# Low parts of the queries formed from the SBUF copy, and one weight split moved a step later, in a one-core decoder step

## What is computed

```python
def nsa_query_side(x, g_pre, w_in):
    u = rms_norm(x, g_pre) @ w_in
    q = u[..., :Q_WIDTH].reshape(b, t, KV_HEADS, GROUP, HEAD_DIM)
    z = u[..., Q_WIDTH:Q_WIDTH * (1 + N_BRANCH)].reshape(b, t, N_BRANCH, N_HEADS, HEAD_DIM)
    gate = jax.nn.sigmoid(u[..., Q_WIDTH * (1 + N_BRANCH):]) ...
    return q, z, gate

# per branch: compressed, selected, window
o = softmax(q k * scale + bias, masked) v          # and y = sum(gate * o * silu(z)) @ w_out
```

## Time and profile before

| | |
|---|---|
| median of three runs | 906.84 us (906.04 to 906.98) |
| span of the profiled execution, first to last instruction | 902.7 us |
| TensorE busy | 870.8 us (96%) |
| VectorE busy | 555.0 us (61%) |
| ScalarE busy | 453.1 us (50%) |
| GpSimd busy | 301.5 us (33%) |
| mean granted TensorE clock | 0.996 |

### The profile page before, as it was taken

One profiled execution on the slowest core, in us unless ns is written; L12 is line 12 of the kernel. 1 busy time (PEld: TensorE's weight loads), 2 busy tenths in 40 slices (PEclk: granted clock), 3 DMA queues, 4 the chain that ended last, 5 costly groups with the idle time before them and its releaser, 6 DMA issues.

```text
span 902.7 us, 16743 instructions
## 1 busy us (share of the span) xinstructions
PE 870.8 (96%) x6226; PEld 754.9 (84%) x6226; DVE 555.0 (61%) x1206; ACT 453.1 (50%) x919; POOL 301.5 (33%) x311
## 2 busy tenths in 40 slices
PE   5999999999999999999999999999999999899996
PEld 4999999946888787779989898989899998786664
DVE  6479999998966772223245555556464645635564
ACT  6567777535544542224446565555564545523231
POOL 2398988797220000003023232323323232500000
PEclk9999999999999999999999999999999999999999
DMA  9365333137178292337323222222322002923521
GB/s 257 97 184 152 102 102 85 40 96 230 42 258 333 107 299 53 105 56 208 95 44 74 48 71 49 70 63 58 69 65 54 25 1 48 276 90 99 184 84 36
DMA packets 158165, 99.52 MB, mean 110 GB/s; under 512 B 97202, under 2 KB 147026, under 8 KB 158005
## 3 DMA queue, kind: packets, MB, share of 16 engines
q1 hardware_dynamic: 143278, 79.30, 32.9%
q0 software_dynamic: 4896, 10.32, 3.2%
q10 hardware_dynamic: 9911, 8.84, 2.9%
HBM read 89.58 MB, written 18.85 MB: 120 GB/s over the span
## 4 chain that ended last, share of the span: by engine, by line
PE 87%; DVE 4%; ACT 4%; issue 3%; ACTq 1%; POOL 1%; DVEq 0%; POOLq 0%
PE psum L2264 8%; PE psum L2265 7%; PE psum L2266 7%; PE psum L1925 6%; PE psum L1927 6%; PE psum L1926 6%; PE psum L2359 6%; PE psum L2117 5%; PE psum L2116 5%; PE psum L2003 5%; PE psum L2118 5%; PE psum L2310 4%; PE psum L2327 3%; PE psum L1906 2%; PE psum L2292 2%
## 5 line engine op out<-in xcount | busy, mean ns | idle before, releaser
L810 ACT ACTIVATE arena<-psum 128x256 f32<-128x256 f32 (+9 forms) x230 | 90.3, 430 | 178.3 <-PE psum L2266 66.2
L2264 PE MATMUL psum<-u_hi,tile_hi 128*128 128x288 f32 x464 | 143.3, 309 | 4.6 <-ACT arena L810 2.2
L789 POOL TENSOR_SCALAR arena<-arena,kept 128x512 f32<-128x512 f32 (+3 forms) x128 | 83.5, 670 | 176.8 <-DVE kept L1762 176.8
L2265 PE MATMUL psum<-u_lo,tile_hi 128*128 128x288 f32 x464 | 137.4, 296 | 0.0
L2266 PE MATMUL psum<-u_hi,tile_lo 128*128 128x288 f32 x464 | 136.4, 294 | 0.0
L1434 DVE SCALAR_TENSOR_TENSOR psum<-arena,psum 128x512 f32<-128x512 f32 x168 | 127.0, 756 | 6.0
L1925 PE MATMUL psum<-h_hi,tile_hi 128*128 128x288 f32 x352 | 104.3, 296 | 0.0
L1926 PE MATMUL psum<-h_lo,tile_hi 128*128 128x288 f32 x352 | 103.8, 295 | 0.0
L1927 PE MATMUL psum<-h_hi,tile_lo 128*128 128x288 f32 x352 | 103.8, 295 | 0.0
L2264 PEld LDWEIGHTS psum<-u_hi,tile_hi 128*128 128x128 f32 x464 | 87.3, 188 | 10.4 <-ACT arena L810 4.1
L1256 ACT ACTIVATE arena<-arena,kept 128x512 f32<-128x512 f32 (+3 forms) x128 | 70.5, 552 | 45.0 <-DVE kept L1728 44.2
(11 more groups left out here) (318 smaller groups left out, 1902.8 us busy)
## 6 DMA issues: line engine op xcount, KB each, us to landing
tile_whole<-in_b_w_in SPq DMA_DIRECT2D x64, 256.0 KB
tile_whole<-in_a_w_in SPq DMA_DIRECT2D x24, 512.0 KB
arena<-in_cmp_w SPq DMA_DIRECT2D x4, 2048.0 KB, 10.3
kvw_whole<-in_w_kv SPq DMA_DIRECT2D x6, 1024.0 KB, 14.2
bias_copies<-bias_line POOLq DMA_DIRECT2D x4, 1280.0 KB, 23.6
arena<-in_x_prompt SPq DMA_DIRECT2D x8, 512.0 KB, 6.4
kvw_whole<-in_a_w_out SPq DMA_DIRECT2D x4, 1024.0 KB, 11.3
arena<-bias_copies SPq DMA_DIRECT2D x16, 256.0 KB, 4.0
```

Of the source, the lines that this page charges most:

```text
L789: pool.tensor_scalar(L, L, rden[:, stat(n) + k:stat(n) + k + 1], gR[:, i, h:h + 1], ALU.mult, ALU.mult).then_inc(S["pn_ready"], 1)
L810: return nc.scalar.activation(out, in_, ACT.Copy, scale=scale)
L2264: pe.matmul(pb(7, HT), w_hi, u_hi[:, k, here], start=(k == 0), stop=False)
L2265: pe.matmul(pb(7, HT), w_hi, u_lo[:, k, here], start=False, stop=False)
```

## The change

Four edits:

- `q_full` moves to another place in SBUF and is 576 columns wide instead of 512, so that it also holds the sampled queries. ScalarE's copy of the second half is 288 columns wide (it was 224). Before it writes, ScalarE also waits until VectorE has finished with the queries of the group before.
- VectorE forms `q_lo` as `q_full - q_hi`, both in SBUF, with a tensor_tensor; it was a scalar_tensor_tensor on bank 7 and `q_hi`. The sampled queries too come from `q_full`.
- `bank_read`: after a half of the queries bank 7 counts as read when ScalarE has written `q_hi`; it counted as read when VectorE had written `q_lo`, and after the second half also the sampled queries.
- The loop that starts `split_lo`: nothing at position 0; at position 1 the split that stood at the end of position 0. The other splits stay.

```diff
-        q_full = at(R_H + 2560, SEQ)
+        q_full = at(R_H + 2432, NT)
...
-            return ("qk_lo", q_low(n, hf)) if kind == "q" else ("zb_ready", 3 * n + (3 if hf else 1))
+            return ("qk_hi", 6 + 2 * (n - 1) + hf + 1) if kind == "q" else ("zb_ready", 3 * n + (3 if hf else 1))
...
                     act.wait_ge(S["s_done"], UPM * (n - 1) + 1)
-                    copy(q_full[:, here], pb(7, here.stop - here.start), QSCALE)
+                    act.wait_ge(S["qk_lo"], q_low(n, 0) - 1)
+                    copy(q_full[:, hf * HT:hf * HT + HT], pb(7, HT), QSCALE)
                     copy(q_hi[:, n % 2, here], pb(7, here.stop - here.start), QSCALE).then_inc(S["qk_hi"], 1)
...
-                q_rest(q_lo[:, m % 2, here], pb(7, here.stop - here.start), q_hi[:, m % 2, here])
+                V.tensor_tensor(out=q_lo[:, m % 2, here], in0=q_full[:, here], in1=q_hi[:, m % 2, here],
+                                op=ALU.subtract).then_inc(S["qk_lo"], 1)
                 if hf:
-                    q_samples(m, pb(7, HT)[:, SEQ - HT:HT], QSCALE)
+                    q_samples(m, q_full[:, SEQ:NT], 1.0)
...
-                for i in tiles_over(n - 1):
+                for i in tiles_over(n - 2) if n % 5 == 1 else tiles_over(n - 1) if n % 5 else ():
                     if i + HRING < N_TILES:
                         split_lo(i + HRING + 1)
```

## The result

The changed kernel takes 920.53 us (median of 5 runs, 920.37 to 923.95) against 906.08 us for the kernel before, in runs on the same chip (5 runs, 903.77 to 906.98). The ratio is 1.0169 (1.015 to 1.0187): slower by 1.7%, clear of its interval, and 1 us beyond the upper end of the predicted range. The profiled spans differ by 15.9 us, where the sum had 9.2. A run's time lies 1.8 us above its span (920.37 against 918.6), not 4.1 us as taken ahead of the prediction; by that, as an estimate, the profiled execution of the kernel before took 904.5 us, 2.3 us under the median of 906.84. The forecast adds to that median and doesn't depend on it.

What follows compares the result with a forecast made beforehand. TensorE, busy 870.8 of 902.7 us, was taken as the bound. Six groups at +1.8 - 0.18 us less 0.5 for group 0 gave +9.2, span 911.9, plus 4.1 to the median: 916.0 us, range 909.5 to 919.5.

Steps and rivals of the forecast that it cites:

- the sum: Whole kernel: +9.7 us for groups 1 to 6 and -0.5 us for group 0, together +9.2 us on the span.
- The bank stops being a limit: Positions 2 and 3, first tile parts: bank 7 clears earlier, saving 0.30 and 0.18 us in each of seven groups.
- TensorE waits six times for the moved split: Sign: TensorE's products of tile 2 wait for VectorE's `tile_lo` six times, about 2 us or more each.
- the addition holds the split: Position 1: the split behind `q_lo` meets GpSimd's addition, lasts about 2.2 us, ends about 1.1 us after it.
- the wait is paid in full: Position 2, first tile part: everything on TensorE stands behind the product awaiting the split, so its whole delay counts, +1.8 us.
- The restart: Position 2: TensorE's start of tile 2, 595.4 against 593.61 before, +1.8 us in each of groups 1 to 6.
- the 0.1 added for the low part: Position 1: 0.1 us added to TensorE's later start because the low part must run in the same place.
- the full series (+2.36): Position 1: low part, addition, split in series behind the last scaling, +2.36 us, 919.4 us; far end of the main case.
- The z gap: Position 1, second tile part: TensorE waits for ScalarE to drain bank 7; closing it saves 0.32 us in six groups.
- the first rival: Position 1: split slips in before GpSimd's addition, takes 1.2 us; 910.7 us (909.8 with shorter low part), chance 0.25.
- The split ahead of the addition: Position 1, same as the first rival: TensorE waits for a split of only 1.2 us, +3.9 us, 910.7 us, chance 0.25.
- The hidden split: Position 2: split ended before TensorE reaches tile 2, so three gaps close, 5.3 us faster, 901.5 us, chance 0.05.

## Why the prediction was wrong

*What held.* TensorE is the bound and only its gaps count. The bank stops being a limit: predicted 0.48 us a group, measured 0.46 with the split back in its old place. TensorE waits six times for the moved split; the addition holds the split to 1.08 us behind its own end. Undoing the one edit gives 903.24 us, doing it alone 924.09.

*The step that failed: "the wait is paid in full".* It charges what stands behind the wait as shifted by the wait and no more, and so takes TensorE's clock as constant. With idle waits of 2.7 us the clock halved in or behind three of six, and the missing term is 5.7 us. With it the sum is 9.2 + 5.7 = 14.9 of the 15.9 us. The two runs with extra matmuls show the cause: the same late split, TensorE idle for 0.34 or 1.52 us only, and the term is gone.

In the projection of the kernel before nothing called a constant clock in question: its gaps around the queries cost 0.2 to 0.3 us each, and the granted clock was 1.00 there. But the first 22 us of the same trace hold a fall that the mean of 0.996 hides. TensorE's row behind the idle time, then two stretches with columns as in the windows above:

```profile
16.84 1.09 PE L1956 MATMUL psum<-kept,arena 128*128 128x128 f32 x8 [1.41 <-POOL arena L712]
```

```profile
15.30:18.70 3.40, 1.99 (x11) 0.96 (x10) 3.40 (x5) 3.39 (x6) 1.48 (x1) 1.00 1.02 227
18.70:22.10 3.40, 3.40 (x15) 3.19 (x15) 3.40 (x8) 2.48 (x5) 0.14 (x1) 0.50 1.15 282
```

TensorE is busy for 1.99 of 3.40 us, and the next 3.40 us run at half clock. No run shows whether the idle 1.41 us or the small products around it brought that fall; it was a reason to give the clock behind the forecast wait a term or a chance, and the prediction gives it neither.

*Terms of the wrong size.* The restart was put at +1.8 us with 0.18 taken off, 1.62 a group; at full clock it is 1.78. The addition took 1.46 us where the earlier trace rows have 1.29, TensorE began 0.14 us behind the split's end and not 0.05, and the 0.1 added for the low part wasn't needed separately: 0.17 + 0.09 - 0.10 = 0.16, the difference. Times six it is the remaining 1 us. The low part took 0.65 us, against 0.46 from PSUM, with the last scaling still running; the full series (+2.36) was too much: it came to 1.78 + 0.18 = 1.96, since the pieces overlap in part. The z gap was worth 0.49 and not 0.32 us: the prediction let the product start 0.08 us ahead of the transposes' end, as behind scores, but without a wait it starts 0.25 ahead of it (594.01 against 593.60 + 0.66 = 594.26). In the changed kernel neither figure counts, for the wait behind it takes the gain back, as forecast. The 909.8 us of the first rival is a slip: with the shorter low part its own terms give 6 x (0.80 - 0.18) - 0.5 = +3.2 us, 910.1; nothing rests on it.

*The rivals.* The split ahead of the addition did not come about by itself, but made to happen its price was right, +0.72 a group. The hidden split did not come about either, since the order put it behind the idle time of VectorE; placed in that idle time it gave 900.75 us, where 901.5 was the rival's price (0.95 us a group, where the price had 0.80, by the z gap).

*Still open.* Why the clock fell for three of six waits (four of six with the split moved alone) and not for the others. The six are equally long (2.71 us, and 2.50 with the split moved alone), so the length of a wait alone doesn't decide it. No run here separates what else differs between them.

## What to carry to other kernels

Work that a critical engine waits for can be moved into its own engine's idle time, but ahead of the instruction that waits there and not behind it: against its old place (ratio 0.9965) the same split cost 2.0% behind `q_lo` (1.0169) and gained 0.3% in front of it (0.9931). When a change makes TensorE stand idle in a busy stretch, for 2.5 to 2.7 us as here, price the clock behind the wait as well as the wait itself, and read the granted clock stretch by stretch, since a mean of 0.989 looks harmless. Two streams from SBUF on VectorE and GpSimd should be costed as taking turns (the same split took 1.21 us away from the addition and 2.28 on it): look for what of the other engine runs at the new place.

## What the runs showed of the hardware

Idle waits of TensorE of 2.7 us inside a busy stretch were followed by 3.40 us at half clock in groups 3 and 5, which costs 1.53 us (the length of group 3 less that of a group at full clock), and in group 1 the clock was at half for 6.83 us, which cost 2.62; three equal waits, in groups 2, 4 and 6, were followed by no fall, nor were the twelve waits of 1.51 to 1.65 us. Only at the start of the kernel, among small products, was a shorter idle time followed by a fall: 1.41 us, then 3.40 us at 0.50, before the change. In group 3 the fall came late: the first eight products after the wait still started 0.13 to 0.21 us apart. In group 1 it came 1.00 us before the wait ended (0.82 on average over the wait). Matmuls whose result is thrown away, issued only to fill the wait, made the changed kernel faster by 0.5 to 0.7% (1.0169 to 1.0115 and 1.0096).
